# Side work of TensorE spread between a chunk's products: transposes, value products, sums, scores, masks and suffix sums issued one or two at a time

## The reference, cut to what matters

```python
proj = rms_norm(h) @ w_in                     # 2048 x 6160, then split by heads
# forgetting attention, a head: scores, decay and mask, softmax, values
logits = einsum('bhqd,bhkd->bhqk', qb, kh) + (cb[..., :, None] - c[..., None, :])
o = einsum('bhqk,bhkd->bhqd', softmax(where(mask, logits, -inf)), vh)
# dilated attention: three patterns, here one softmax with counts (value products and sums)
# PEER: every expert's u = down @ x is worked out densely: (gate * gelu(x @ down.T)) @ up
# second block: window attention with relative bias and a sink column, and
z = einsum('bqhd,bshd->bhqs', q_blk, k) * D ** -0.5              # stick-breaking
between = lax.cumsum(log_1m_beta, axis=3, reverse=True) - log_1m_beta
o = einsum('bhqs,bshd->bqhd', where(strict, exp(log_beta + between), 0.0), v)
x = x + square(relu(h @ w1)) @ w2
```

## Time and profile before

| | us |
|---|---|
| median of 3 runs (3115.39 to 3116.09) | 3116.03 |
| the profiled execution, its own time | 3111.83 |
| its span, first to last instruction | 3110.0 |
| TensorE busy | 3073.7 (99%), 14724 matmuls |
| weight loads busy | 2609.2 (84%) |
| VectorE, ScalarE, GpSimd busy | 1773.8, 1464.2, 638.3 |
| mean granted TensorE clock | 0.996 |

### The profile page before, as it was taken

One profiled execution on the slowest core, in us unless ns is written; L12 is line 12 of the kernel. 1 busy time (PEld: TensorE's weight loads), 2 busy tenths in 40 slices (PEclk: granted clock), 3 DMA queues, 4 the chain that ended last, 5 costly groups with the idle time before them and its releaser, 6 DMA issues. The chain is left out here.

```text
span 3110.0 us, 40502 instructions
## 1 busy us (share of the span) xinstructions
PE 3073.7 (99%) x14724; PEld 2609.2 (84%) x14724; DVE 1773.8 (57%) x2339; ACT 1464.2 (47%) x1822; POOL 638.3 (21%) x455
## 2 busy tenths in 40 slices
PE   8999999999999999999999999999999999999998
PEld 7999888888888888888888888899888888888886
DVE  5445554689864444565565556645776454545444
ACT  5444454554544444444444444554565444444453
POOL 3110000088888887000000000000000000000000
PEclk9999999999999999999999999999999999999999
DMA  6764467688888778777776775654446666666664
GB/s 217 244 203 135 136 202 253 194 217 217 216 218 221 214 219 249 272 238 239 238 230 212 226 250 182 190 181 147 127 140 186 187 191 189 189 190 187 191 186 148
DMA packets 215975, 627.60 MB, mean 202 GB/s; under 512 B 58139, under 2 KB 58789, under 8 KB 215472
## 3 DMA queue, kind: packets, MB, share of 16 engines
q1 hardware_dynamic: 156544, 549.79, 56.8%
q0 software_dynamic: 54464, 59.30, 7.7%
q10 hardware_dynamic: 4848, 16.94, 1.4%
HBM read 587.78 MB, written 38.14 MB: 201 GB/s over the span
## 5 line engine op out<-in xcount | busy, mean ns | idle before, releaser
L571 DVE TENSOR_TENSOR w_lo<-raw,w_hi 128x1024 fp32r<-128x1024 f32 (+2 forms) x1072 | 1280.0, 1196 | 1167.5 <-ACT w_hi L566 1164.7
L566 ACT ACTIVATE w_hi<-raw 128x1024 fp32r<-128x1024 f32 (+2 forms) x1072 | 1106.6, 1034 | 1342.0 <-PE ps L1612 1034.0
L1610 PE MATMUL ps<-w_hi,a_hi 128*128 128x512 f32 x1536 | 601.4, 392 | 0.0
L1612 PE MATMUL ps<-w_hi,a_lo 128*128 128x512 f32 x1536 | 598.1, 389 | 0.0
L1611 PE MATMUL ps<-w_lo,a_hi 128*128 128x512 f32 x1536 | 597.8, 389 | 0.0
L1610 PE MATMUL ps<-w_hi,x_hi 128*128 128x512 f32 x1504 | 587.3, 390 | 0.0
L1612 PE MATMUL ps<-w_hi,x_lo 128*128 128x512 f32 x1504 | 585.4, 389 | 0.0
L1611 PE MATMUL ps<-w_lo,x_hi 128*128 128x512 f32 x1504 | 585.2, 389 | 0.0
L468 POOL DMA_INDIRECT gates<-srch x256 | 518.4, 2025 | 151.3 <-issue 77.5
L1761 PE MATMUL ps<-w_hi,x_hi 128*128 128x440 f32 (+2 forms) x1184 | 450.4, 380 | 2.4 <-DVE x_lo L1046 2.4
L1763 PE MATMUL ps<-w_hi,x_lo 128*128 128x440 f32 (+2 forms) x1184 | 438.1, 370 | 0.0
(11 more groups left out here) (336 smaller groups left out, 1714.3 us busy)
## 6 DMA issues: line engine op xcount, KB each, us to landing
raw<-in_peer_down SPq DMA_DIRECT2D x256, 512.0 KB
raw<-in_peer_up SPq DMA_DIRECT2D x256, 512.0 KB
raw<-in_w_mlp_in SPq DMA_DIRECT2D x128, 512.0 KB
raw<-in_w_mlp_out SPq DMA_DIRECT2D x128, 512.0 KB
raw<-in_w_in SPq DMA_DIRECT2D x112, 440.0 KB
raw<-in_w_in SPq DMA_DIRECT2D x96, 428.0 KB
raw<-in_w_out SPq DMA_DIRECT2D x64, 512.0 KB
gates<-zero POOLq DMA_DIRECT2D x32, 512.0 KB, 4.8
```

Of the source, the lines that this page charges most:

```text
L566: act.activation(w_hi[:, c % RING, 0:2 * n], raw[:, c % RING, 0:2 * n], ACT.Copy).then_inc(hi_made, 1)
L571: nc.vector.tensor_tensor(w_lo[:, c % RING, 0:2 * n], raw[:, c % RING, 0:2 * n], w_hi[:, c % RING, 0:2 * n].bitcast(F32), ALU.subtract).th ...
L1610: mm(o, xh, wh, start=(k == 0), stop=False)
L1612: last = mm(o, xl, wh, start=False, stop=(k == KT - 1))
```

## The change

`between(m)` is called after each of a chunk's 12 products (m = 0 to 11), and every side function takes `m` and issues only its m-th instruction (the two heads' scores together, a head's decay terms and mask together). What stood as a group behind chunk s now stands inside chunk s + 1, from behind its first product on: `beside1` and `beside2` call the functions for `s - 1`. Their waits come at m = 0. `x_turn` 8 to 15 and `x_turn2` before chunk 117 take the slots m = 6 to 9. The eight transposes of `turn_hidden` and `turn_back` go into the last eight slots (m = 4 to 11) of the chunk that they stood behind. The gated linear attention (`gla`), the key scores, and the first eight `x_turn` stay behind their chunks. `chunk_used` is still given by the chunk's last product. No other engine's order changes.

```diff
+                        m = 6 * kk + 3 * t
                         mm(o, xh, wh, start=(k == 0), stop=False)
+                        if between:
+                            between(m)
                         mm(o, xh, wl, start=False, stop=False)
+                        if between:
+                            between(m + 1)
                         last = mm(o, xl, wh, start=False, stop=(k == KT - 1))
-                last.then_inc(chunk_used, 1)
+                        if m == 9:
+                            last.then_inc(chunk_used, 1)
+                        if between:
+                            between(m + 2)
 
...
+                def turn_hidden(r, i, m):
+
+                    if m == 0:
+                        pe.wait_ge(copied_out, acts + 4 * r + i + 1)
+                        free = h0 + 4 * r + i - 1
+                        if not static(free) or free > 0:
+                            pe.wait_ge(hid_lo, free)
+                    if 0 <= m < 8:
+                        jj, t = divmod(m, NT)
+                        ins = pe.transpose(ps[:, 4 + 2 * (i % 2) + jj // 2, (jj % 2) * S + t * P:(jj % 2) * S + t * P + P],
+                                           hid[:, t, jj * P:jj * P + P], ident)
+                        if m == 7:
+                            ins.then_inc(hid_turned, 1)
 
...
+            def score_pair(n, m):
+
+                if m == 0:
+                    pe.wait_ge(qk_copied, n + 1)
+                    if n:
+                        pe.wait_ge(exp_made, n)
+                    else:
+                        pe.wait_ge(masks_made, 2)
+                        pe.wait_ge(c_split, 1)
...
+                        pe.wait_ge(row_copied, 1)
+                if m < 6:
+                    t, j = divmod(m, 3)
+                    at, w = ((0, P), (P, S))[t]
+                if m in (0, 3):
                     for j in range(2):
                         at_ = slice(HD * j, HD * j + HD)
                         mm(ps[:, 6 + j, at:at + w], qkT[at_, t * P:t * P + P], qkT[at_, S:S + w], start=True, stop=False)
-                    for j in range(2):
-                        o, f = ps[:, 6 + j, at:at + w], 2 * n + j
-                        if n < FOX_PAIRS:
-                            mm(o, c_parts[:, 0, t * P:t * P + P], pick[:, f, 0:w], start=False, stop=False)
-                            mm(o, pick[:, f, 0:P], c_parts[:, 1, 0:w], start=False, stop=False)
-                            last = mm(ps[:, 6 + j, at + w - P:at + w], ident_b[:], caus, start=False, stop=True)
-                        else:
-                            last = mm(o, ident_b[:], mask_b[:, at:at + w], start=False, stop=True)
-                last.then_inc(scored, 1)
-
...
+            def beside1(s):
+
+                turns = 2 + sum(at < s - 1 for at in XTURN_AT[2:])
+
+                def between(m):
+                    for n, at in enumerate(PAIR_AT):
+                        if s - 1 == at + 1:
+                            score_pair(n, m)
+                        if s - 1 == at + 5:
+                            pv_pair(n, m)
+                        if s - 1 == at:
+                            turn_pair(n, turns, m)
+                        if s - 1 == at + 3:
+                            turn_pair_p(n, turns, m)
+                    for j, at in enumerate(XTURN_AT):
+                        if s - 1 == at and j >= 8:
+                            x_turn(j, m if j >= 16 else m - 6)
+                return between
+
             for s, (name, b, c) in enumerate(SEQ):
                 if name == "in1":
...
+            def x_turn2(s, m):
 
                 for j, (at, g, bank_, col) in enumerate(XTURN2):
...
+            def score_swa(n, m):
                 g = PAIRS + n
-                pe.wait_ge(qk_copied, g + 1)
-                pe.wait_ge(exp_made, g)
-                for t, at, w in ((0, 0, P), (1, P, S)):
+                if m == 0:
+                    pe.wait_ge(qk_copied, g + 1)
+                    pe.wait_ge(exp_made, g)
+                if m < 2:
+                    at, w = ((0, P), (P, S))[m]
                     for j in range(2):
                         at_ = slice(HD * j, HD * j + HD)
-                        last = mm(ps[:, 6 + j, at:at + w], qkT[at_, t * P:t * P + P], qkT[at_, S:S + w], start=True, stop=True)
-                last.then_inc(scored, 1)
-
-            def pv_swa(n):
+                        ins = mm(ps[:, 6 + j, at:at + w], qkT[at_, m * P:m * P + P], qkT[at_, S:S + w], start=True, stop=True)
+                    if m == 1:
+                        ins.then_inc(scored, 1)
+
...
+            def beside2(s):
+
+                turns = 24 + sum(x[0] < s - 1 for x in XTURN2)
+
+                def between(m):
+                    for n, at in enumerate(SWA_AT):
+                        if s - 1 == at + 1:
+                            score_swa(n, m)
+                        if s - 1 == at + 5:
+                            pv_swa(n, m)
+                        if s - 1 == at:
+                            turn_swa(n, turns, m)
+                        if s - 1 == at + 3:
+                            turn_pair_p(PAIRS + n, turns, m)
+                    for n, at in enumerate(SB_AT):
+                        if s - 1 == at + 1:
+                            score_sb(n, m)
+                        if s - 1 == at + 5:
+                            sums_sb(n, turns, m)
+                        if s - 1 == at + 8:
+                            pv_sb(n, m)
+                        if s - 1 == at:
+                            turn_sb(n, turns, m)
+                    x_turn2(s - 1, m if s > 116 else m - 6)
+                return between
+
             for s, (name, b, c) in enumerate(SEQ2):
                 i = s // SUB
                 if name == "in2":
```

More of the change, by code:

```diff
@@ L1672, in x_turn @@
                     pe.wait_ge(x_lo_made, j)
-                for kk in range(2):
-                    k = 2 * (j % 8) + kk
-                    for t in range(NT):
-                        last = pe.transpose(ps[:, XTURN_BANK[j], kk * S + t * P:kk * S + t * P + P], src[:, t, k * P:k * P + P], ident)
-                last.then_inc(x_turned, 1)
             def pair_cols(n):
@@ new lines, in turn_pair_p @@
+            def turn_pair_p(n, turns, m):
+                if m == 0:
+                    pe.wait_ge(exp_made, n + 1)
+                    pe.wait_ge(x_lo_made, turns)
+                    if n:
+                        pe.wait_ge(head_out, n)
+                if m < 6:
+                    j, b = divmod(m, 3)
+                    ins = pe.transpose(ps[:, 4 + j, b * P:b * P + P], prob[:, j, b * P:b * P + P], ident)
+                    if m == 5:
+                        ins.then_inc(p_turned, 1)
@@ L1754, in part @@
+            def part(s, name, b, c, parity, n, hi, lo, first, last_c, between):
                 pe.wait_ge(lo_made, s + 1)
@@ L1800, in _ @@
                         pe.wait_ge(x_lo_made, 16 + c + 1)
-                    part(s, name, b, c, b % 2, WIDE, x_hi, x_lo, 0, 7)
-                turns = 2 + sum(at < s for at in XTURN_AT[2:])
+                    part(s, name, b, c, b % 2, WIDE, x_hi, x_lo, 0, 7, beside1(s))
                 if s == 12:
@@ L1931, in x_turn2 @@
-                    pe.wait_ge(x_lo_made, 24 + j - (1 if j >= 1 and XTURN2[j - 1][2] != bank_ else 0))
-                    for kk in range(2):
-                        k = 2 * g + kk
-                        for t in range(NT):
-                            last = pe.transpose(ps[:, bank_, kk * S + t * P:kk * S + t * P + P], src[:, t, k * P:k * P + P], ident)
-                    last.then_inc(x_turned, 1)
-            def open2(pos):
-                x_turn2(pos - 32)
-            phase(True, 8, 7, True, False, open2)
+                    if m == 0:
+                        x_turn2_waits(s, j, g, bank_)
@@ new lines, in x_turn2, with x_turn2_waits @@
+                    if 0 <= m < 4:
+                        k, t = 2 * g + m // NT, m % NT
+                        ins = pe.transpose(ps[:, bank_, m * P:m * P + P], (mix if 8 <= j < 16 else h)[:, t, k * P:k * P + P], ident)
+                        if m == 3:
+                            ins.then_inc(x_turned, 1)
+            def x_turn2_waits(s, j, g, bank_):
+                if j < 8:
+                    pe.wait_ge(added_out, after("peer")[2] - 3 + g // 2)
+                    pe.wait_ge(hid_lo, 4 * PEER_ROUNDS)
+                elif j < 16:
+                    if 3 <= g < 6:
+                        pe.wait_ge(gla_out, NT)
+                    else:
+                        pe.wait_ge(head_out, PAIRS + {0: 2, 1: 4, 2: 6, 6: 8, 7: 10}[g])
+                    pe.wait_ge(p_copied, PAIRS + SWA_PAIRS)
+                    pe.wait_ge(head_out, PAIRS + SWA_PAIRS)
+                    pe.wait_ge(qk_copied, PAIRS + SWA_PAIRS + sum(p_ <= s for p_ in SB_AT))
+                    pe.wait_ge(sb_add, sum(p_ + 5 <= s for p_ in SB_AT))
+                else:
```

(28 more changed lines are left out.)

397 lines of the change are left out of this document (184 added, 213 removed).

## The result

| | us |
|---|---|
| before, median of 6 runs beside it | 3115.31 (3113.67 to 3116.09) |
| after, median of 6 runs | 3132.06 (3129.25 to 3133.44) |
| ratio | 1.0054, 95% interval 1.0042 to 1.0065 |
| profiled execution after, span | 3127.4 (before 3110.0) |

What follows compares the result with a forecast made beforehand. TensorE, busy 3073.7 of 3110.0 us, bounds the kernel. Transposes +5, scores +8.8, waits +3.6 and clock -1.2 sum to +16.2 us, taking the 3116.0 median to 3132, range 3118 to 3143.

Steps and rivals of the forecast that it cites:

- transposes at 512 columns: 512-column stages: a fixed cost per change between transpose and product, 0.012 us for 580 more changes; +5 us, bounds 0 to 10.
- scores: Half-row score products of all pairs: full-row products between them make TensorE switch twice, not once; +8.8 us, bounds 0 to 12.
- sixth forgetting pair: First block: the output its transposes need is ready just before they start and hangs on that pair's scores; +1.0 us.
- other waits: Window softmaxes +0.2, first suffix sums +1.5, chunk 98 +0.9, behind `sums_sb` +0.5, shrunk `x_turn` waits -0.5 us.
- clock: Dilated pairs: with value products spread between products, the fall in granted clock should not come; -1.2 us.
- rival A: Short matmuls on TensorE: the weight load behind one hides after all between products, making the kernel faster; 5%.
- 428 and 440 columns at nothing: Stages with products of 428 and 440 columns: spreading full-row work there costs nothing.
- the first suffix sums: Second block: `x_turn2` of chunks 90 to 93 end ten products later and ScalarE waits for each; +1.5 us.
- Chunk 98: TensorE waits 1.9 us for `x_lo` ahead of the value products instead of 0.85 behind them; +0.9 us.
- C: Second block: stretched tight chains make waits take over at four to six places, with lower clock; +30 us, 3146; 10%.
- B: Whole kernel: no measurable change, as half-row switches hide behind a product in flight; -1 to +6 us, say 3119; 14%.
- D: Whole kernel slightly faster: clock and shrunk waits give 3 us more than counted, scores half; 3113 or less; 3%.

Runs made afterwards that it cites:

- e1: Kernel before with only the transposes of `turn_hidden` and `turn_back` spread behind a chunk's products, one or two at a time; 3117.5 us, ratio 1.0002 to 1.0020.
- e11: Kernel before with only `turn_hidden` and `turn_back` spread, two transposes in each of four slots; 3116.1 us, ratio 0.9998 to 1.0016.
- e3: Kernel after, but each score group issued whole behind the next chunk's first product; 3123.4 us, ratio 1.0016 to 1.0040.
- e7: Kernel after, but `x_turn` of chunks 8 to 15 and `x_turn2` up to chunk 116 in slots 0 to 3, not 6 to 9; 3125.7 us.
- e4: Kernel after, but side groups issued whole behind the next chunk's first product, `turn_hidden` and `turn_back` behind their own chunks; 3116.1 us, ratio 0.9997 to 1.0015.
- e8: Kernel before with only the value products of forgetting and dilated pairs spread behind the next chunk's products; 3114.1 us, ratio 0.9993 to 1.0012.
- e2: Kernel before with only the scores spread over the slots of the next chunk; 3129.2 us, ratio 1.0035 to 1.0063.
- e6: Kernel before, but forgetting and dilated pairs issue the 128-column part's bf16 terms first, then all score products, then the other terms; 3110.1 us, ratio 0.9976 to 0.9994.
- e9: Kernel e6 with the first block's value products spread too; 3109.6 us, ratio to before 0.9976 to 0.9994.

## Why the prediction was right, and where it was lucky

The parts, by stages and runs, against the prediction's:

| | forecast | measured | from |
|---|---|---|---|
| transposes at 512 columns | +5 | +3.6 | e1, e11 |
| scores | +8.8 | +8.0, of which 6.3 in their own chunks | after less e3, without the sixth pair's wait |
| sixth forgetting pair | +1.0 | +1.1 | its wait in after, absent in e3 |
| other waits; measured with all that is left | +2.6 | +4.9 | e7 3.5, e4 0.6, rest 0.8 |
| clock | -1.2 | -2.2 | estimated cost of the stretches at 0.50, 5.6 and 3.4 us |
| sum | +16.2 | +15.4 (+16.7 by the medians) | the two profiled executions, without the first nine chunks |

- **The load behind a short matmul is not hidden**, alone or in a group: right, 0.111 to 0.117 against 0.11. It was what decided between the forecast and rival A; what a hidden load would have been worth, no run shows. The rows show one load ahead and no second.
- **The fixed part at 512 columns.** It does belong to the change between product and transpose, as e1 and e11 show. I took 5 out of 0 to 10 and it is 3.6. The price of 0.012 us for each change was right (0.009 and 0.011); my count of 580 changes was too high a base for it, since e1's 48 groups make 336 of them and account for all of the 3.6.
- **428 and 440 columns at nothing.** A single transpose costs 0.111 to 0.113 there and not 0.109, so about 0.003 a slot were lost. e8 has value products spread alone: 1.4 us by the stages, of which I had counted nothing.
- **Scores.** The price of a visit was right where it stands alone: window pairs +0.40 and forgetting pairs +0.41 or more in e2, forecast 0.41 and 0.36. In the full kernel it is not paid at ten pairs of the first block, which cost 0.03 to 0.08 each: I had 0.7 for all that value products hide, and by the 0.3 that is missing at each of these pairs it is some 3 us. The visits so come to 6.3 us and not 8.8. That the term as a whole is 8.0 is luck, for waits behind the scores, which I had not counted there, filled it up.
- **Waits.** This term was the one mis-sized most: 3.6 with the sixth pair, 6.0 measured (with the 0.8 that no run assigns, and without those that e3 took away with the scores). The late transposes of x cost 3.5, and "the first suffix sums, +1.5" had only half: beside their wait (3.0 before, 4.2 after) there is the second ones' of 1.8, a chain at which I had not looked. Chunk 98 waited the 1.9 us that were forecast, but chunks 784 to 787 grew by 2.3 in the kernel after and 1.6 in e4, not 0.9. I had seen that the six value products would now stand behind the wait, and took 0.9 for wait and products together. The waits for window softmaxes shrank (6.7 to 5.5), most likely since TensorE arrives later there by more than the scores end later; no run parts this.
- **Clock.** The fall near 384 went: 1.5 to 1.7 us. No run shows the 1.2 of the forecast, which I took from too narrow a window. The rest of the -2.2 is the stretch at 2210, half as long (0.65, since TensorE waited through much of it). That is not to be put down to the change: among the kernels with before's order in the second block, e6 has 6.8 us at 0.50 there, and before, e1, e8, e9 and e11 have 10.2.
- **The profiled execution.** I compared sums with a trace that lay 4.2 us below the median and took the difference of the two as the same for both kernels. 1.9 us of it was a shorter start, which no later trace has. It did no harm, since the forecast was put on the median.

The errors in waits (+2.4), the slots at 512 columns (-1.4), the scores (-0.8) and the clock (-1.0) cancelled to 1 us. The rivals: A is out by the weight loads above, C by the list of waits (three long new ones, 4.8 us in all, where it wanted 30), B and D by the switches that e2, e3 and e6 show.

## What to carry to other kernels

Where TensorE is full, look at what stands next to what. A short matmul cost its successor's weight load here (0.11 us) alone as in a group, so scattering it brought nothing; each visit to half rows has a price of its own (0.3 to 0.4 us here, though next to nothing where short full-row matmuls shared the slots), so keep such matmuls together and put the full-row work on either side. When a group is cut up, its last piece comes later by the products between: follow every chain that hangs on that last piece, past the first wait that it meets, before giving the cut a price.

## What the runs showed of the hardware that was not expected

- A single transpose between long products is slower than one in a row (0.117 against 0.110 at 512 columns, 0.111 against 0.109 at 428), and the product behind it starts 0.03 us after it.
- The same order of instructions had a granted clock of 0.50 for 6.8 us of the second block in one execution and for 10.2 in another (e6 and before), in pieces of 3.4 us, most of them in or behind TensorE's longest waits (before: from 2210.0, in the wait of 4.4 us, and from 2271.4, at the end of the one of 3.0). In the first block it came only in the six kernels with grouped value products of 64 and 2 columns, in the kernel before without any wait ahead of it (TensorE busy 3.40 of 3.40 us).
- The stages of the profiled executions repeat to 0.03 us between kernels where no order differs, in hundreds of chunks at a time, so a stage's difference tells 0.3 us where the medians tell some 2, as long as no stretch at 0.50 falls into it.
